# Two 256-column products in place of one 512-column product, per weight tile, in a float32 transformer trunk

## The chip, the cores and the metric

The kernel runs on one core of one Trainium2 chip. The metric is the device time of one execution in microseconds (us), lower is better. TensorE (PE) multiplies, and a matmul needs its stationary tile loaded first (the trace shows these loads as PEld). VectorE (DVE) and ScalarE (ACT) do the elementwise work, GpSimd (POOL) and SyncE (SP) issue the DMAs.

## The reference

Two decoder layers over 256 tokens of width 2048, all in float32. Layer 0 mixes tokens with attention with forget gates (16 heads of 128), layer 1 with a gated convolution of width 3. Each mixer is followed by a squared-ReLU MLP of width 8192, and each sub-layer has an RMSNorm, a shift and scale and a residual gate, which come from a conditioning vector `c`.

```python
for i in range(DEPTH):
    mod = c_act @ ada_w[i] + ada_b[i]
    sh_mix, sc_mix, g_mix, sh_mlp, sc_mlp, g_mlp = jnp.split(mod, N_MOD, axis=-1)
    h = modulate(rmsnorm(x, norm_mix[i]), sh_mix, sc_mix)
    mix = fox_mixer(...) if i % 2 == 0 else short_conv_mixer(...)
    x = x + g_mix[:, None, :] * mix
    h = modulate(rmsnorm(x, norm_mlp[i]), sh_mlp, sc_mlp)
    x = x + g_mlp[:, None, :] * sq_relu_mlp(h, mlp_w_up[i], mlp_w_down[i])
return rmsnorm(x, final_norm)
```

## The kernel before

All weights stream once from memory, so the matmuls are cut into 96 units. A unit is the product of 2048 input rows with 512 output columns of some weight matrix: 12 units for q, k and v, 4 for the attention output, 32 for the first MLP (4 slices of 4 up and 4 down units), 12 and 4 for the convolution mixer, 32 for the second MLP. Activations lie transposed, with features on the partitions and the 256 tokens in the columns.

To keep float32 accuracy with a faster number format (float32r), each number is split in a rounded high part and a low rest. For a weight chunk of 2 x 128 rows, ACT writes the high part (`w_hi`, line 598) and DVE the rest (`w_lo`, line 773). The ring of these chunks is four deep, and a unit has eight of them (`e` runs over them). The activations (`h`, `mid`) hold both parts side by side, 256 columns of the high part and then 256 of the low one. For each of the 16 k-steps of a unit and each of its 4 blocks of 128 output columns, `multiply` has two matmuls: `hi` times all 512 columns into a whole PSUM bank (line 370), and `lo` times the 256 high columns into the first half of this bank (line 372). That makes hi·hi + lo·hi in columns 0 to 255 and hi·lo in columns 256 to 511. These two are called the pair below. Four of the q, k, v units (v) are laid out the other way round, with `tokens_out`, and have three 512-column matmuls (lines 363 to 365).

The two halves of a bank are put together at the end of the unit. ACT copies the second half of its four banks to `tmp` (`half`, line 615, 1024 columns), and DVE adds it to the first half (`whole`, line 828 or 830). After this comes what the unit needs: the residual (ACT applies the gate, DVE adds to `xT`, ACT squares, DVE sums the squares), the squared ReLU, or the convolution. Two sets of four PSUM banks alternate, so that TensorE begins unit u when unit u-2 has been read (`evacuated`). ACT and DVE each have one order written out by hand, `body`: eight splits for the chunks ahead, between them pieces of the matrix-vector product with `ada_w` (DVE, line 785), then the evacuation. The first chunks of unit u+1 are split before unit u is evacuated.

The attention's own matmuls have up to 256 columns: `scores` (lines 486 to 490, ten matmuls for each head, of 256 and 128 columns) and `mix_values` (lines 509 to 511, six for each head). In both, one stationary tile is in part used by two matmuls in a row.

Of the kernel before, what the change touches and what calls it, by code (L numbers as in the profile page):

```python
# [1 line left out]

# [21 lines left out]
T = 256  # L24
# [42 lines left out]
def build(nc, x, c, ada_w, ada_b, norm_mix, norm_mlp, fox_w_in, fox_b_f, fox_w_out,  # L67
          conv_w_in, conv_w, conv_w_out, mlp_w_up, mlp_w_down, final_norm, out):
    ctx = ExitStack()
    with ctx:  # L70
# [103 lines left out]
        hi_ready = sem("hi_ready")  # L174
        split_ready = sem("split_ready")
        split_used = sem("split_used")
        half_ready = sem("half_ready")
        evacuated = sem("evacuated")
        ada_steps = sem("ada_steps")
        ada_summed = sem("ada_summed")  # L180
# [164 lines left out]
        def _(pe):  # L345
            mm = nc.tensor.matmul

            def multiply(u, par, rhs, ada=None, tokens_out=False, ready=None, after=None):


                pe.wait_ge(evacuated, u + 1)
                for e in range(NE):
                    pe.wait_ge(split_ready, NE * u + e + NE + 1)
                    if ready is not None:
                        ready(e)
                    for kk in range(EK):
                        k = EK * e + kk
                        hi, lo = w_hi[:, e % WR, kk, :], w_lo[:, e % WR, kk, :]
                        if tokens_out:
                            for a in range(TT):  # L360
                                o = ps[:, NB * par + a, :]
                                xh, xl = rhs[:, k, 0, P * a:P * (a + 1)], rhs[:, k, 1, P * a:P * (a + 1)]
                                mm(o, xh, hi, start=(k == 0), stop=False)  # L363
                                mm(o, xl, hi, start=False, stop=False)
                                last = mm(o, xh, lo, start=False, stop=(k == KC - 1))
                        else:
                            for j in range(NB):
                                cols = slice(P * j, P * (j + 1))

                                mm(ps[:, NB * par + j, :], hi[:, cols], rhs[:, k, :, :].rearrange("p s t -> p (s t)"),  # L370
                                   start=(k == 0), stop=False)
                                last = mm(ps[:, NB * par + j, 0:T], lo[:, cols], rhs[:, k, 0, :],  # L372
                                          start=False, stop=(k == KC - 1))
                    last.then_inc(split_used, 1)
                    if e == NE // 2 - 1 and ada is not None:
                        pe.wait_ge(evacuated, u + 2)

                        ada_sum(*ada, NB * par + NB - 1 if tokens_out else NB * (1 - par))
                    if after is not None and e in after:
                        after[e]()  # L380
# [209 lines left out]
        def _(act):  # L590
# [18 lines left out]
                act.wait_ge(split_used, NE * u + NE)  # L609
                evac()  # L610

            def half(u, par, scale=1.0, n_red=NQ):
                act.wait_ge(evacuated, u + 2)
                act.wait_ge(reduced, n_red)
                op(tmp, ps[:, NB * par:NB * (par + 1), T:2 * T], ACT.Copy, scale=scale).then_inc(half_ready, 1)  # L615

            def residual(u, par, gate0, k, n_res):
                half(u, par, n_red=NQ + n_res)
                act.wait_ge(evacuated, u + 3)
                for j in range(NB):  # L620
# [72 lines left out]
            for g in range(NG):  # L693
                for t in range(3):
                    u = 3 * g + t
                    par = u % 2

                    def evac():
                        if t == 2:
                            op(vs[:, :, 0, :], ps[:, NB * par:NB * par + TT, :], ACT.Copy).then_inc(qkv_hi, 1)  # L700
                        else:
                            half(u, par, SCALE if t == 0 else 1.0)
                            act.wait_ge(evacuated, u + 3)
                            op((qs, ks)[t][:, :, 0, :], fsum, ACT.Copy).then_inc(qkv_hi, 1)
                            if t == 1:
                                load_nf(g)
                    after = None
                    if t == 0 and g:
                        after = {1: lambda: round_attn(g - 1, NB * (1 - par) + 2)}
                    elif t == 1 and g == 0:  # L710
                        after = {1: forget_rows}
                    elif t == 2:
                        after = {0: lambda: exps(g, NB * (1 - par)), 2: lambda: round_probs(g, NB * (1 - par))}
                    body(u, evac, after=after)
# [4 lines left out]
            def mlp_slice(s, base, l, last=False):  # L719
                for n in range(NG):  # L720
                    u = base + 2 * NG * s + n

                    def evac():
                        half(u, n % 2, n_red=NQ + NG * (1 + l) + SLICES * NG * l + NG * s)
                        act.wait_ge(relu2, SLICES * NG * l + NG * s + n + 1)
                        op(mid[:, NB * n:NB * (n + 1), 0, :], fsum, ACT.Copy).then_inc(hid_hi, 1)  # L726
                    body(u, evac)
                for n in range(NG):
                    u = base + 2 * NG * s + NG + n
                    body(u, lambda: residual(u, n % 2, NROW * l + 5 * KC, NB * n,  # L730
                                             NG * (1 + l) + SLICES * NG * l + NG * s + n), more=not (last and n == NG - 1))
# [5 lines left out]
            with act.Fori(0, NG // 2) as r:  # L737
                for i in range(2):
                    g = 2 * r + i
                    for t in range(3):  # L740
# [1 line left out]
                        u = U_CONV + 6 * r + pos  # L742

                        def evac():
                            half(u, pos % 2, n_red=NQ + NG * (1 + SLICES))
                            if t == 2:
                                act.wait_ge(conv_in, g + 1)
                                act.wait_ge(conv_ready, g)
                                for j in range(NB):
                                    last = op(conv_y[:, j, :], conv_u[:, j, 0:T], ACT.Copy, scale=taps[:, ds(NB * g + j, 1)])  # L750
                                last.then_inc(conv_tap, 1)
                                act.wait_ge(conv_gated, g + 1)
                                op(mid[:, ds(NB * g, NB), 0, :], conv_y[:, :, :], ACT.Copy).then_inc(conv_hi, 1)
# [14 lines left out]
        def _(dve):  # L768
# [50 lines left out]
                for i in range(ada_late, NQ):  # L819
                    ada_quarter_of(i)  # L820

            def whole(u, par, dst, scale=1.0, n_half=None, used=()):

                for wait in used:
                    dve.wait_ge(*wait)
                dve.wait_ge(half_ready, n_half)
                if scale == 1.0:
                    v.tensor_tensor(dst, ps[:, NB * par:NB * (par + 1), 0:T], tmp, ALU.add).then_inc(evacuated, 1)  # L828
                else:
                    v.scalar_tensor_tensor(dst, ps[:, NB * par:NB * (par + 1), 0:T], scale, tmp,  # L830
                                           ALU.mult, ALU.add).then_inc(evacuated, 1)

            def residual(u, par, k, slot, n_half, n_res, used=()):
                whole(u, par, fsum, n_half=n_half, used=((added, n_res),) + used)
                dve.wait_ge(gated, n_res + 1)
                v.tensor_tensor(xT[:, ds(k, NB), :], xT[:, ds(k, NB), :], fsum, ALU.add).then_inc(added, 1)  # L836

# [171 lines left out]
            for g in range(NG):  # L1009
                for t in range(3):  # L1010
# [3 lines left out]
                    def evac():  # L1014
# [3 lines left out]
                                            vs[:, :, 0, :].bitcast(F32), ALU.subtract).then_inc(evacuated, 1)  # L1018
                        else:
                            dst = (qs, ks)[t]  # L1020
                            whole(u, par, fsum, SCALE if t == 0 else 1.0, n_half=2 * g + t + 1,
                                  used=((qkv_ready, 2 * g + t),))
                            dve.wait_ge(qkv_hi, 3 * g + t + 1)
                            v.tensor_tensor(dst[:, :, 1, :], fsum, dst[:, :, 0, :].bitcast(F32), ALU.subtract).then_inc(qkv_ready, 1)
# [10 lines left out]
                         ada_first=t == 2, ada_late=2 if t == 1 else NQ)  # L1035
            for n in range(NG):
                u = U_OUT0 + n
                body(u, lambda: residual(u, n % 2, NB * n, n, u - NG + 1, n),
                     (u + A_START, n % 2), (u + A_START - 1, NB * ((n + 1) % 2)),
                     after=None if n else {1: lambda: low_attn(NG - 1, NB + 2)})  # L1040

            def mlp_slice(s, base, l, adas, last=False):
                n_hid = SLICES * NG * l + NG * s
                n_add = NG * (1 + l) + n_hid
                for n in range(2 * NG):
# [2 lines left out]

                    def evac():
                        if n >= NG:  # L1050
                            residual(u, n % 2, NB * (n - NG), n - NG, u - NG + 1, n_add + n - NG, ((hid_ready, n_hid + NG),))
                            return
                        whole(u, n % 2, fsum, n_half=u - NG + 1, used=((hid_ready, n_hid + n), (added, n_add)))
                        dve.wait_ge(evacuated, u + 3)
                        v.scalar_tensor_tensor(fsum, fsum, 0.0, fsum, ALU.max, ALU.mult).then_inc(relu2, 1)  # L1055
                        dve.wait_ge(hid_hi, n_hid + n + 1)
# [14 lines left out]
            with dve.Fori(0, NG // 2) as r:  # L1071
                for i in range(2):
                    g = 2 * r + i
                    for t in range(3):
# [2 lines left out]
                        a = A_CONV + 4 * r + 2 * i + t  # L1077

                        def evac():
                            whole(u, pos % 2, (conv_b[:, :, :], conv_c[:, :, :], fsum)[t], n_half=u - NG + 1)  # L1080
                            if t == 2:
                                dve.wait_ge(evacuated, u + 3)
                                v.tensor_tensor(conv_u[:, :, 2:T + 2], conv_c[:, :, :], fsum, ALU.mult).then_inc(conv_in, 1)
# [12 lines left out]
                        body(u, evac, (a, t % 2) if t < 2 else None, (a - 1, NB * ((pos + 1) % 2)) if t else None)  # L1096
            for n in range(NG):
                u = U_OUT1 + n
                body(u, lambda: residual(u, n % 2, NB * n, n, u - NG + 1, NG * (1 + SLICES) + n))
            norm(3, MLP_GAIN[1], NROW + 3 * KC, A_END)  # L1100
            with dve.Fori(0, SLICES - 1) as s:
                mlp_slice(s, U_MLP1, 1, False)
# [28 lines left out]
```

## Time and profile before

| | |
|---|---|
| median of 3 runs | 2579.46 us (2575.14 to 2583.95) |
| span of the profiled execution | 2578.3 us, first to last instruction |
| PE busy | 2382.4 us, 92% |
| DVE busy | 1923.0 us, 75% |
| ACT busy | 1102.4 us, 43% |
| mean granted TensorE clock | 0.950 of full speed |
| read from memory | 606 MB, 236 GB/s over the span |

Durations of matmuls overlap in the trace: a matmul's record lasts until its results are written, and the next one has long begun. What a matmul costs in a stream is therefore the time from its start to the next one's start, which is called its step below. The profiled execution's own total time isn't given beside its span; its span lies 1.2 us under the median of the runs.

### The profile page before, as it was taken

What the parts mean: (1) busy time and instruction counts of PE and PEld (TensorE: products, weight loads), DVE (VectorE), ACT (ScalarE), POOL (GpSimd) and SP (SyncE); (2) the same over time, 40 slices, a digit from 0 to 9 for tenths busy, and PEclk for the clock granted to TensorE, in tenths of its full rate; (3) what the DMA queues carried; (4) which work ended last, traced back from release to release, by engine and by line L of the source; (5) the groups of instructions that cost most, each with busy time, mean ns of one, the idle gap of its engine ahead of it and who ended that gap; (6) DMA issues with size and microseconds to landing.
All of it is one profiled execution on the core that took longest, in us unless ns stands there. A gap on an engine that the chain in (4) does not pass through costs nothing.

```text
span 2578.3 us, 35741 instructions
## 1 busy us (share of the span) xinstructions
PE 2382.4 (92%) x13304; PEld 2075.5 (80%) x13304; DVE 1923.0 (75%) x2089; ACT 1102.4 (43%) x1252; POOL 148.3 (6%) x208
## 2 busy tenths in 40 slices
PE   4899998985999999999997999998899999999996
PEld 4887787774888888888886888887788888888885
DVE  6878889888877887887888888865756555565555
ACT  1044434434444454444444344344445445445452
POOL 2201011100000000000000000000000000000000
PEclk7589999997999999999998999999999999999998
DMA  8967798884887877878874887755455555655551
GB/s 306 340 240 271 273 323 297 279 292 165 287 282 253 271 271 265 277 262 271 271 270 162 315 298 271 265 177 194 130 181 188 179 173 196 187 189 180 185 175 66
DMA packets 259228, 610.80 MB, mean 237 GB/s; under 512 B 11656, under 2 KB 12024, under 8 KB 258816
## 3 DMA queue, kind: packets, MB, share of 16 engines
q1 hardware_dynamic: 206768, 407.18, 46.8%
q0 software_dynamic: 52224, 201.34, 22.5%
q8 instruction: 114, 1.87, 0.3%
q14 instruction: 42, 0.34, 0.0%
q10 hardware_dynamic: 80, 0.07, 0.0%
HBM read 606.42 MB, written 2.13 MB: 236 GB/s over the span
## 4 chain that ended last, share of the span: by engine, by line
PE 74%; DVE 14%; issue 4%; ACT 4%; DMA 3%; DVEq 0%; SPq 0%; ACTq 0%; POOLq 0%
PE ps L370 46%; PE ps L372 23%; DVE acc L785 5%; DMA ada_raw<-in_ada_w_dram 3%; DVE w_lo L773 3%; PE ps L438 1%; DVE scratch L828 1%; PE ps L386 1%; ACT w_hi L598 1%; DVE squares L843 1%; ACT scratch L621 1%; DVE scratch L948 1%; DVE h L956 1%; ACT h L649 1%; DMA xrow<-in_x_dram 1%
## 5 line engine op out<-in xcount | busy, mean ns | idle before, releaser
L370 PE MATMUL ps<-h,w_hi 128*128 128x512 f32 x3328 | 1189.7, 402 | 63.6 <-DVE h L956 22.5
L773 DVE TENSOR_TENSOR w_lo<-raw,w_hi 128x1024 fp32r<-128x1024 f32 x768 | 916.8, 1221 | 372.2 <-ACT w_hi L598 367.9
L598 ACT ACTIVATE w_hi<-raw 128x1024 fp32r<-128x1024 f32 x768 | 797.8, 1057 | 896.3 <-PE ps L372 894.9
L372 PE MATMUL ps<-h,w_lo 128*128 128x256 f32 x3328 | 939.2, 282 | 0.0
L370 PE MATMUL ps<-mid,w_hi 128*128 128x512 f32 x2560 | 908.9, 399 | 16.0 <-DVE w_lo L773 14.5
L370 PEld LDWEIGHTS ps<-h,w_hi 128*128 128x128 f32 x3328 | 633.5, 190 | 222.1 <-issue 46.7
L372 PE MATMUL ps<-mid,w_lo 128*128 128x256 f32 x2560 | 720.8, 282 | 0.0
L372 PEld LDWEIGHTS ps<-h,w_lo 128*128 128x128 f32 x3328 | 636.9, 191 | 0.0
L370 PEld LDWEIGHTS ps<-mid,w_hi 128*128 128x128 f32 x2560 | 484.1, 189 | 134.4 <-DVE w_lo L773 15.1
L372 PEld LDWEIGHTS ps<-mid,w_lo 128*128 128x128 f32 x2560 | 486.9, 190 | 0.0
L785 DVE SCALAR_TENSOR_TENSOR acc<-ada_raw,ca,acc 128x512 f32<-128x512 f32 x600 | 450.6, 751 | 34.6 <-DMA ada_raw<-in_ada_w_dram 17.0
L336 POOL DMA_DIRECT2D ada_raw<-in_ada_w_dram x160 | 120.4, 752 | 1450.6 <-DVE acc L785 1412.6
L843 DVE TENSOR_REDUCE squares<-scratch 128x256 f32<-128x1024 f32 x44 | 88.7, 2017 | 48.4 <-ACT scratch L624 45.1
L828 DVE TENSOR_TENSOR scratch<-ps,scratch 128x1024 f32<-128x1024 f32 x80 | 97.5, 1218 | 9.6 <-ACT scratch L615 9.6
L621 ACT ACTIVATE scratch<-scratch,mod 128x256 f32<-128x256 f32 x160 | 68.4, 498 | 81.7 <-DVE scratch L828 81.7
L836 DVE TENSOR_TENSOR xT<-xT,scratch 128x1024 f32<-128x1024 f32 x40 | 49.0, 1226 | 71.0 <-ACT scratch L621 71.0
L615 ACT ACTIVATE scratch<-ps 128x1024 f32<-128x1024 f32 x92 | 92.7, 1008 | 10.2 <-PE ps L372 10.2
L785 DVE SCALAR_TENSOR_TENSOR acc<-start_ring,ca,acc 128x512 f32<-128x512 f32 x90 | 67.6, 752 | 6.9 <-DMA start_ring<-in_ada_w_dram 2.8
L726 ACT ACTIVATE mid<-scratch 128x1024 fp32r<-128x1024 f32 x32 | 34.0, 1062 | 88.8 <-DVE scratch L1055 88.8
L649 ACT ACTIVATE h<-scratch 128x512 fp32r<-128x512 f32 x32 | 20.2, 632 | 110.9 <-DVE scratch L948 110.9
L363 PE MATMUL ps<-w_hi,h 128*128 128x512 f32 x128 | 53.7, 420 | 14.1 <-DVE w_lo L773 14.1
L395 PE MATMUL ps<-squares,ones 128*128 128x256 f32 x40 | 16.5, 546 | 54.2 <-DVE squares L843 45.8
(138 smaller groups left out, 1078.0 us busy)
## 6 DMA issues: line engine op xcount, KB each, us to landing
ada_raw<-in_ada_w_dram POOLq DMA_DIRECT2D x160, 1024.0 KB, 6.3
raw<-in_mlp_w_up_dram SPq DMA_DIRECT2D x128, 1024.0 KB, 5.6
raw<-in_mlp_w_down_dram SPq DMA_DIRECT2D x128, 1024.0 KB, 5.3
raw<-in_fox_w_in_dram SPq DMA_DIRECT2D x48, 1024.0 KB, 7.3
raw<-in_conv_w_in_dram SPq DMA_DIRECT2D x48, 1024.0 KB, 7.6
start_ring<-in_ada_w_dram POOLq DMA_DIRECT2D x32, 1024.0 KB, 9.1
raw<-in_fox_w_out_dram SPq DMA_DIRECT2D x16, 1024.0 KB, 7.5
raw<-in_conv_w_out_dram SPq DMA_DIRECT2D x16, 1024.0 KB, 5.2
```

Source lines behind the costliest of these rows:

```text
L336: pool.dma_start(ada_raw[:, q % 2], ada_quarter(layer, a - NMOD * NG * layer, q)).then_inc(ada_arrived[q % 2], 16)
L363: mm(o, xh, hi, start=(k == 0), stop=False)
L370: mm(ps[:, NB * par + j, :], hi[:, cols], rhs[:, k, :, :].rearrange("p s t -> p (s t)"), start=(k == 0), stop=False)
L372: last = mm(ps[:, NB * par + j, 0:T], lo[:, cols], rhs[:, k, 0, :], start=False, stop=(k == KC - 1))
L598: op(w_hi[:, e % WR], raw[:, e // 2, EK * (e % 2):EK * (e % 2 + 1)], ACT.Copy).then_inc(hi_ready, 1)
L615: op(tmp, ps[:, NB * par:NB * (par + 1), T:2 * T], ACT.Copy, scale=scale).then_inc(half_ready, 1)
L621: last = op(fsum[:, j, :], fsum[:, j, :], ACT.Copy, scale=mod[:, ds(gate0 + k + j, 1)])
L773: v.tensor_tensor(w_lo[:, e % WR], raw[:, e // 2, EK * (e % 2):EK * (e % 2 + 1)], w_hi[:, e % WR].bitcast(F32), ALU.subtract).then_inc(spl ...
L785: v.scalar_tensor_tensor(acc[:, slot, :], src[:, kk, :], ca[:, k:k + 1], acc[:, slot, :], ALU.mult, ALU.add).then_inc(ada_steps, 1)
L828: v.tensor_tensor(dst, ps[:, NB * par:NB * (par + 1), 0:T], tmp, ALU.add).then_inc(evacuated, 1)
L836: v.tensor_tensor(xT[:, ds(k, NB), :], xT[:, ds(k, NB), :], fsum, ALU.add).then_inc(added, 1)
L843: v.tensor_reduce(squares[:, m, :], tmp.rearrange("p k t -> p t k"), AX.X, ALU.add).then_inc(reduced, 1)
```

## The change

The 512-column matmul becomes two matmuls of 256 columns with the same stationary tile, both into columns 0 to 255. All three products are then summed in PSUM, in the same half of the bank; the other half is unused. `half` is gone with its semaphore, and `whole` reads the one half by itself and writes it out, times `scale`.

```diff
-  mm(ps[:, NB * par + j, :], hi[:, cols], rhs[:, k, :, :].rearrange("p s t -> p (s t)"),
-     start=(k == 0), stop=False)
+  mm(ps[:, NB * par + j, 0:T], hi[:, cols], rhs[:, k, 0, :], start=(k == 0), stop=False)
+  mm(ps[:, NB * par + j, 0:T], hi[:, cols], rhs[:, k, 1, :], start=False, stop=False)
   last = mm(ps[:, NB * par + j, 0:T], lo[:, cols], rhs[:, k, 0, :],
             start=False, stop=(k == KC - 1))
...
-  def half(u, par, scale=1.0, n_red=NQ):
-      act.wait_ge(evacuated, u + 2)
-      act.wait_ge(reduced, n_red)
-      op(tmp, ps[:, NB * par:NB * (par + 1), T:2 * T], ACT.Copy, scale=scale).then_inc(half_ready, 1)
...
   def residual(u, par, gate0, k, n_res):
-      half(u, par, n_red=NQ + n_res)
       act.wait_ge(evacuated, u + 3)
...
-  def whole(u, par, dst, scale=1.0, n_half=None, used=()):
+  def whole(u, par, dst, scale=1.0, used=()):
       for wait in used:
           dve.wait_ge(*wait)
-      dve.wait_ge(half_ready, n_half)
-      if scale == 1.0:
-          v.tensor_tensor(dst, ps[:, NB * par:NB * (par + 1), 0:T], tmp, ALU.add).then_inc(evacuated, 1)
-      else:
-          v.scalar_tensor_tensor(dst, ps[:, NB * par:NB * (par + 1), 0:T], scale, tmp,
-                                 ALU.mult, ALU.add).then_inc(evacuated, 1)
+      dve.wait_ge(split_used, NE * u + NE)
+      v.tensor_scalar(dst, ps[:, NB * par:NB * (par + 1), 0:T], scale, None, ALU.mult).then_inc(evacuated, 1)
```

The calls of `half` in the four evacuations of ACT and the argument `n_half` in those of DVE go with it. The four `tokens_out` units are unchanged.

## Rows read from the trace of the kernel before

**Rows 1.** Page, busy time: engine, us (share), instructions.

```profile
span 2578.3 us, 35741 instructions
...
PE 2382.4 (92%) x13304; PEld 2075.5 (80%) x13304; DVE 1923.0 (75%) x2089; ACT 1102.4 (43%) x1252; POOL 148.3 (6%) x208
```

**Rows 2.** Page, the chain that ended last, by line.

```profile
PE ps L370 46%; PE ps L372 23%; DVE acc L785 5%; DMA ada_raw<-in_ada_w_dram 3%; DVE w_lo L773 3%; PE ps L438 1%; DVE scratch L828 1%; PE ps L386 1%; ACT w_hi L598 1%; DVE squares L843 1%; ACT scratch L621 1%; DVE scratch L948 1%; DVE h L956 1%; ACT h L649 1%; DMA xrow<-in_x_dram 1%
```

**Rows 3.** Groups by line and shape: xcount, busy us, mean ns, idle before.

```profile
L370 PE MATMUL ps<-h,w_hi 128*128 128x512 f32 x3328 | 1189.7, 402 | 63.6 <-DVE h L956 22.5 <-DVE w_lo L773 22.3 <-issue 8.3
L370 PE MATMUL ps<-mid,w_hi 128*128 128x512 f32 x2560 | 908.9, 399 | 16.0 <-DVE w_lo L773 14.5 <-issue 1.5
...
L828 DVE TENSOR_TENSOR scratch<-ps,scratch 128x1024 f32<-128x1024 f32 x80 | 97.5, 1218 | 9.6 <-ACT scratch L615 9.6
...
L848 DVE TENSOR_SCALAR var<-ps 128x256 f32<-128x256 f32 x5 | 2.1, 423 | 7.5 <-PE ps L395 7.5
...
L853 DVE TENSOR_TENSOR newton<-inv 128x256 f32<-128x256 f32 x5 | 2.1, 426 | 2.4 <-ACT inv L640 1.9 <-ACT inv L634 0.5
...
L615 ACT ACTIVATE scratch<-ps 128x1024 f32<-128x1024 f32 x92 | 92.7, 1008 | 10.2 <-PE ps L372 10.2
```

**Rows 4.** Line 370 alone in four stretches: A:B, us, PE busy (count), PEld busy (count), clock, DMA.

```profile
650.00:800.00 150.00, 147.70 (x421) 78.77 (x421) 1.00 0.82 280
1220.00:1370.00 150.00, 147.71 (x422) 78.90 (x421) 1.00 0.80 270
1850.00:1990.00 140.00, 140.00 (x397) 74.46 (x397) 1.00 0.56 183
2210.00:2310.00 100.00, 100.00 (x289) 54.03 (x289) 1.00 0.57 184
```

**Rows 5.** PE's timeline, the pair in the stream: start us, duration us.

```profile
1200.24 0.40 PE L370 MATMUL ps<-h,w_hi 128*128 128x512 f32 x1
...
1200.48 0.28 PE L372 MATMUL ps<-h,w_lo 128*128 128x256 f32 x1
...
1200.59 0.40 PE L370 MATMUL ps<-h,w_hi 128*128 128x512 f32 x1
```

**Rows 6.** PE's timeline, attention scores of head group 3.

```profile
461.71 0.33 PE L486 MATMUL ps<-ks,qs 128*128 128x256 f32 x1
...
462.40 0.27 PE L487 MATMUL ps<-ks,qs 128*128 128x128 f32 x1
...
462.73 0.28 PE L490 MATMUL ps<-causal,ident_r 128*128 128x128 f32 x1
...
463.99 0.33 PE L486 MATMUL ps<-ks,qs 128*128 128x256 f32 x1
```

**Rows 7.** PE's timeline, attention values of head group 3.

```profile
500.77 0.34 PE L509 MATMUL ps<-qs,vs 128*128 128x256 f32 x1
...
502.14 0.45 PE L370 MATMUL ps<-mid,w_hi 128*128 128x512 f32 x1
```

**Rows 8.** PE's timeline in a v unit, only 512-column matmuls, ten steps apart.

```profile
470.36 0.39 PE L363 MATMUL ps<-w_hi,h 128*128 128x512 f32 x1
...
472.63 0.39 PE L364 MATMUL ps<-w_hi,h 128*128 128x512 f32 x1
```

**Rows 9.** ACT's and DVE's timeline around the end of one unit.

```profile
789.17 1.06 ACT L598 ACTIVATE w_hi<-raw 128x1024 fp32r<-128x1024 f32 x1 [1.71 <-PE ps L372]
790.14 1.01 ACT L615 ACTIVATE scratch<-ps 128x1024 f32<-128x1024 f32 x1
...
790.27 1.23 DVE L773 TENSOR_TENSOR w_lo<-raw,w_hi 128x1024 fp32r<-128x1024 f32 x1 [0.16 <-ACT w_hi L598]
791.41 1.22 DVE L828 TENSOR_TENSOR scratch<-ps,scratch 128x1024 f32<-128x1024 f32 x1
```

**Rows 10.** Timeline after the last unit.

```profile
2545.96 1.02 ACT L615 ACTIVATE scratch<-ps 128x1024 f32<-128x1024 f32 x1 [10.25 <-PE ps L372]
```

**Rows 11.** Waits: who waited for whom, us in total, times, longest.

```profile
PE ps L370 <- DVE w_lo L773: 36.9, 11, 4.3
...
PE ps L370 <- DVE scratch L828: 7.6, 2, 3.9
```

More of the change, by code:

```diff
@@ L176, in build @@
         split_used = sem("split_used")
-        half_ready = sem("half_ready")
         evacuated = sem("evacuated")
@@ L701, in evac @@
                         else:
-                            half(u, par, SCALE if t == 0 else 1.0)
                             act.wait_ge(evacuated, u + 3)
@@ L723, in evac @@
                     def evac():
-                        half(u, n % 2, n_red=NQ + NG * (1 + l) + SLICES * NG * l + NG * s)
                         act.wait_ge(relu2, SLICES * NG * l + NG * s + n + 1)
@@ L744, in evac @@
                         def evac():
-                            half(u, pos % 2, n_red=NQ + NG * (1 + SLICES))
                             if t == 2:
@@ L820, in body, with residual @@
                     ada_quarter_of(i)
-            def whole(u, par, dst, scale=1.0, n_half=None, used=()):
+            def whole(u, par, dst, scale=1.0, used=()):
                 for wait in used:
                     dve.wait_ge(*wait)
-                dve.wait_ge(half_ready, n_half)
-                if scale == 1.0:
-                    v.tensor_tensor(dst, ps[:, NB * par:NB * (par + 1), 0:T], tmp, ALU.add).then_inc(evacuated, 1)
-                else:
-                    v.scalar_tensor_tensor(dst, ps[:, NB * par:NB * (par + 1), 0:T], scale, tmp,
-                                           ALU.mult, ALU.add).then_inc(evacuated, 1)
-            def residual(u, par, k, slot, n_half, n_res, used=()):
-                whole(u, par, fsum, n_half=n_half, used=((added, n_res),) + used)
+                dve.wait_ge(split_used, NE * u + NE)
+                v.tensor_scalar(dst, ps[:, NB * par:NB * (par + 1), 0:T], scale, None, ALU.mult).then_inc(evacuated, 1)
+            def residual(u, par, k, slot, n_res, used=()):
+                whole(u, par, fsum, used=((added, n_res),) + used)
                 dve.wait_ge(gated, n_res + 1)
@@ L1020, in evac @@
                             dst = (qs, ks)[t]
-                            whole(u, par, fsum, SCALE if t == 0 else 1.0, n_half=2 * g + t + 1,
+                            whole(u, par, fsum, SCALE if t == 0 else 1.0,
                                   used=((qkv_ready, 2 * g + t),))
@@ L1037, in _ @@
                 u = U_OUT0 + n
-                body(u, lambda: residual(u, n % 2, NB * n, n, u - NG + 1, n),
+                body(u, lambda: residual(u, n % 2, NB * n, n, n),
                      (u + A_START, n % 2), (u + A_START - 1, NB * ((n + 1) % 2)),
@@ L1050, in evac @@
                         if n >= NG:
-                            residual(u, n % 2, NB * (n - NG), n - NG, u - NG + 1, n_add + n - NG, ((hid_ready, n_hid + NG),))
+                            residual(u, n % 2, NB * (n - NG), n - NG, n_add + n - NG, ((hid_ready, n_hid + NG),))
                             return
-                        whole(u, n % 2, fsum, n_half=u - NG + 1, used=((hid_ready, n_hid + n), (added, n_add)))
+                        whole(u, n % 2, fsum, used=((hid_ready, n_hid + n), (added, n_add)))
                         dve.wait_ge(evacuated, u + 3)
@@ L1079, in evac @@
                         def evac():
-                            whole(u, pos % 2, (conv_b[:, :, :], conv_c[:, :, :], fsum)[t], n_half=u - NG + 1)
+                            whole(u, pos % 2, (conv_b[:, :, :], conv_c[:, :, :], fsum)[t])
                             if t == 2:
@@ L1098, in _ @@
                 u = U_OUT1 + n
-                body(u, lambda: residual(u, n % 2, NB * n, n, u - NG + 1, NG * (1 + SLICES) + n))
+                body(u, lambda: residual(u, n % 2, NB * n, n, NG * (1 + SLICES) + n))
             norm(3, MLP_GAIN[1], NROW + 3 * KC, A_END)
```

## The prediction

> **What bounds the kernel.** I read the busy shares first, then the chain that ended last, then the groups by line, and last the timelines, because the records of matmuls overlap and their durations say little. PE is busy for 92% of the span and no other engine for more than 80% [rows 1]; the chain lies on the pair of lines 370 and 372 for 69% of the span [rows 2]. There are 3328 + 2560 = 5888 pairs [rows 3]. So the question is what one pair costs in the stream, and what three shorter matmuls cost in its place. All else is small against 5888 times a few nanoseconds: 1 ns per pair is 5.9 us, and a difference of 0.3%, about what a measurement of this kernel can tell from none, is 7.7 us or 1.3 ns per pair.
>
> **What a pair costs.** In four stretches at full granted clock line 370 began 421, 422, 397 and 289 times in 147.7, 147.7, 140.0 and 100.0 us of its own busy time, which for an overlapping stream is the time it fills [rows 4]. That is 0.351, 0.350, 0.353 and 0.346 us per pair. All four together: 535.4 / 1529 = 0.350 us. There are two paces, 0.353 (third stretch) and 0.346 (fourth), and nothing in their DMA share (0.56 and 0.57) tells them apart. 768 columns at one column per cycle of 2.4 GHz are 0.320 us, so 26 to 33 ns of a pair aren't columns. In the timeline the 512-column matmul takes a step of 0.24 and the 256-column one of 0.11 [rows 5].
>
> **What the change adds on PE.** Per pair, one matmul and one weight load more, with the same 768 columns: 5888 matmuls and 5888 loads more. Loads stand one to one beside matmuls before (13304 of each, rows 1), also where two in a row have the same tile, so the second half's load isn't saved. The third matmul is free only if all that lies between two matmuls is hidden behind columns. The cost is that of three steps of 256 columns. I take it from the places where 256-column matmuls follow each other:
>
> - Scores: two heads' worth, from 461.71 to 463.99, hold 2 x 10 matmuls, 2 x 4 of 256 columns and 2 x 6 of 128; per head 1.140 us. Three steps between 128-column matmuls take 462.73 - 462.40 = 0.33, so 0.110 each, or 0.112 with the rounding of the rows [rows 6]. (1.140 - 6 x 0.112) / 4 = 0.117, and with 0.110 it is 0.120.
> - Values: from 500.77 to 502.14 there are two heads of 3 + 3 matmuls, 0.685 per head [rows 7]. (0.685 - 3 x 0.112) / 3 = 0.116; with 0.110 it is 0.118. Here the order is the changed one: high tile, high tile again, low tile.
>
> I take 0.118, in the middle of 0.116 to 0.120, because these are the same operation with the same tile sizes. Three of them are 0.354 us, against 0.350: +4 ns per pair.
>
> Both bounds are far. Below: a 128-column matmul with its load takes 0.110 [rows 6], more than twice its columns' 0.053, so it is the load or the issue that sets it, and nothing goes below this; three are 0.330, -20 ns per pair or -118 us. Above: ten 512-column steps take 2.27 us, 0.227 each [rows 8], 13.7 ns over their columns. If each matmul had this whatever its size, three would cost 0.320 + 0.041 = 0.361, +11 ns; with the pair's own excess at its slower pace, 33 ns / 2 = 16.7 per matmul, it would be 0.370, +20 ns or +118 us. The short step of line 372 in the pair, 0.11 to 0.12 [rows 5], would make 0.345, -5 ns, but part of that step may be booked to its neighbour of 0.24.
>
> Here a rule can be laid beside the row. The row says that a 512-column matmul takes 0.227 us in a stream [rows 8]. The Trainium skill, page "TensorE: Matmul & The Clock Gate", section "Back-to-back issue gap", gives columns / 2.4 plus 2.5 ns, so 0.216, which the row exceeds by 11 ns. By the page one more matmul per pair would cost 2.5 ns or +15 us, as an estimate; its section on loading the stationary operand gives 107 ns for 128 columns, as long as a 256-column matmul's columns, which speaks against this change, since such a load has no spare cover. The trace agrees with the load's figure: 0.110 a step at 128 columns.
>
> **How many pairs pay.** Where PE waits for DVE's `w_lo` in any case, slower matmuls eat into the wait. There are 11 such waits of 36.9 us together [rows 11], one for one unit each; I take half of the 64 pairs of each as covered, 350. 5888 - 350 = 5540 pairs x 4 ns = +22 us.
>
> **What it removes.** 92 copies on ACT of 1.008 us [rows 3], 92.7 us of work, but beside the path. At the end of a unit ACT first does the last split (to 790.23), then the copy (790.14 to 791.15), while DVE splits the same chunk (790.27 to 791.50) and only then adds (791.41) [rows 9]. The copy is done before DVE could use it. All adds together have waited 9.6 us for the copy, once [rows 3]: after the last unit, where there are no further splits. There the copy of 1.02 us is on the path [rows 10] and goes away: -1 us. At nothing I cost the other 91, hidden by DVE's own split; without this cover they would cost 1 us each on the residual chain. ACT has 57% idle time, so its freed time isn't needed.
>
> The add becomes a scaling of 1024 columns out of PSUM on DVE. At 256 columns a `TENSOR_SCALAR` from PSUM takes 423 ns and a `TENSOR_TENSOR` 426 [rows 3], so I take the same 1.22 us and 0 for the difference; should it run shorter, it would be 92 times some tenths, off the path in the MLP units. Its wait moves from the copy to the last matmul of the unit, which is earlier. Behind it on DVE are the splits of the next unit, and they gain nothing since DVE comes to it late.
>
> `evacuated` comes no later, so PE's wait for a free bank (7.6 us in two waits, rows 11) stays. More instructions on PE must be fetched after each loop's jump; I put that at +0 to +3 us and leave it out of the sum.
>
> **Sum.** +22 - 1 = +21 us. The span would go from 2578.3 to 2599; the median of the runs is 1.2 us above the span, so 2600 us.
>
> **The rivals.**
>
> 1. *A fixed price per matmul.* If handing over from one stationary tile to the next costs as much at 256 columns as at 512, a triple is 0.360 to 0.370 and the time 2579 + (10 to 17 ns x 5888 = 59 to 100) = 2640 to 2680. For it speaks that 512-column steps (13.7 ns over) and the pair (26 to 33 over for two matmuls) fit the same price; against it that 256-column steps in attention are only 10 to 13 over. Also in this class: the attention's runs are 40 matmuls long, and a sustained stream of 17 loads and matmuls per us, where the pair has 11, is shown nowhere; if PE can't be fed at this rate for long, it costs here.
> 2. *Short steps (faster).* In the pair the 256-column matmul's step is 0.11 to 0.12, and what hangs over may belong to the 512-column one. If all three take 0.115, a triple is 0.345, and the time 2579 - 5 x 5888 = 2550. It decides below 0.1167 (0.350 / 3). For it speaks row group 5; against it that in attention, where sums over whole heads leave nothing to be booked to a neighbour, I find 0.116 to 0.120.
> 3. *Columns alone count.* The excess is in proportion to the columns: 0.350 / 768 per column, the triple costs what the pair costs, and only the copy at the end is left: 2575 to 2586. Rows 8 speak against it: 0.227 for 512 columns is less per column than the pair.
>
> **How the numbers follow.** Forecast (triple 0.352 to 0.357, +10 to +40 us) 0.42; rival 1 0.20; rival 2 0.21; rival 3 0.17. Slower is 0.42 + 0.20 = 0.62, faster 0.21, the same 0.17. The predicted time is 2600, its own range 2589 to 2619. The range for 8 in 10 takes in rival 3, rival 2 down to 2552 and the lower part of rival 1, to 2655; outside are 0.08 of rival 2 and 0.10 of rival 1.
>
> **What the profile after would show.** PE with 13304 + 5888 = 19192 matmuls and as many loads. In the stream, one step of about 0.118 after the other and 0.354 per block of three; 0.345 shows rival 2, 0.360 and more rival 1. ACT's busy time down by 93 us, DVE's unchanged within 5 us with the new group at 1.2 us. The evacuation begins at the same distance from the unit's last matmul as before, except after the last unit, where it comes 1 us sooner. I would be wrong in kind if the stalls between units changed by more than some us in sum.

## The result, and the profile after

The changed kernel takes 2656.8 us (2654.4 to 2658.7, 4 runs) against 2581.1 (2575.1 to 2584.0) of the kernel before: slower by 3.1%, ratio 1.0308, 95% interval 1.0285 to 1.033. The way was forecast; the size, +21 us, was less than a third of the 76 us measured, and 2656.8 lies just over the range of 2552 to 2655. The span went from 2578.3 to 2654.9 us, +76.6.

The page of the changed kernel: busy time, then the chain that ended last by line, then groups by line (what each writes and reads, count, busy us, mean ns, idle time before).

```profile
span 2654.9 us, 47284 instructions
...
PE 2444.0 (92%) x19192; PEld 2410.0 (91%) x19192; DVE 1924.6 (72%) x2089; ACT 1017.4 (38%) x1160; POOL 147.8 (6%) x208
...
PE ps L359 25%; PE ps L360 25%; PE ps L361 25%; DVE acc L765 3%; DMA ada_raw<-in_ada_w_dram 2%; PE ps L427 1%; DVE scratch L807 1%; PE ps L375 1%; ACT w_hi L587 1%; DVE w_lo L753 1%; DVE squares L819 1%; DVE scratch L924 1%; DVE h L932 1%; ACT h L632 1%; DMA xrow<-in_x_dram 1%
...
L359 PE MATMUL ps<-h,w_hi 128*128 128x256 f32 x3328 | 959.5, 288 | 72.7 <-issue 29.5
L360 PE MATMUL ps<-h,w_hi 128*128 128x256 f32 x3328 | 955.4, 287 | 9.0 <-issue 9.0
...
L807 DVE TENSOR_SCALAR scratch<-ps 128x1024 f32<-128x1024 f32 x84 | 102.3, 1218 | 8.9 <-PE ps L361 8.9
```

The three matmuls are now lines 359 to 361, `whole` is line 807. PE has the 19192 matmuls and as many loads. VectorE is unchanged in sum, and its new evacuation takes 1.218 us like the add that it replaces [rows 3]; ACT has lost the 92 copies. The chain lies on the three matmuls for 75% of a longer span. Two things have grown against [rows 1, 3]: the weight loads are busy for 91% of the span, nearly as long as the matmuls, where it was 80%, and idle time named "issue" before the matmuls is 29.5 + 9.0 us, where it was 8.3 + 1.5.

The stream itself, PE's timeline:

```profile
2622.75 0.28 PE L359 MATMUL ps<-mid,w_hi 128*128 128x256 f32 x1
2622.87 0.28 PE L360 MATMUL ps<-mid,w_hi 128*128 128x256 f32 x1
...
2622.99 0.28 PE L361 MATMUL ps<-mid,w_lo 128*128 128x256 f32 x1
...
2623.11 0.28 PE L359 MATMUL ps<-mid,w_hi 128*128 128x256 f32 x1
...
2623.23 0.28 PE L360 MATMUL ps<-mid,w_hi 128*128 128x256 f32 x1
```

Every step is 0.120, and three are 0.360 us. The two paces of the pair [rows 4] are gone.

And one jump back of TensorE's loop over the slices, in the second MLP. First the kernel before, then the changed one (timeline of PE; the square bracket is the idle time before):

```profile
1997.71 0.28 PE L372 MATMUL ps<-mid,w_lo 128*128 128x256 f32 x1
1998.97 0.47 PE L370 MATMUL ps<-h,w_hi 128*128 128x512 f32 x1 [0.98 <-issue]
...
2001.97 0.50 PE L370 MATMUL ps<-h,w_hi 128*128 128x512 f32 x1 [1.03 <-issue]
```

```profile
2043.43 0.55 PE L359 MATMUL ps<-h,w_hi 128*128 128x256 f32 x1 [4.67 <-issue]
...
2045.07 0.41 PE L360 MATMUL ps<-h,w_hi 128*128 128x256 f32 x1
2045.28 0.41 PE L361 MATMUL ps<-h,w_lo 128*128 128x256 f32 x1
2045.49 0.41 PE L359 MATMUL ps<-h,w_hi 128*128 128x256 f32 x1
2049.19 0.58 PE L360 MATMUL ps<-h,w_hi 128*128 128x256 f32 x1 [3.28 <-issue]
```

2.0 us of idle time at this jump have become 8.0, in two parts, and the steps between are 0.21: TensorE is at the lower of its two clocks, 1.2 GHz. Four stretches of 23 us of the changed kernel show what that makes (A:B, us, busy and count of PE, PEld, DVE, ACT, POOL, granted clock, DMA): one without a jump, and the three that hold a jump of the second MLP.

```profile
1998.00:2021.00 23.00, 23.00 (x194) 23.00 (x193) 13.81 (x12) 10.91 (x13) 0.00 (x0) 1.00 0.55 180
2038.00:2061.00 23.00, 15.04 (x101) 14.57 (x100) 9.38 (x8) 6.99 (x9) 0.00 (x0) 0.78 0.32 97
2233.00:2256.00 23.00, 15.66 (x108) 15.19 (x107) 9.84 (x8) 6.99 (x9) 0.00 (x0) 0.78 0.35 108
2428.00:2451.00 23.00, 15.56 (x107) 15.09 (x107) 9.55 (x8) 7.12 (x10) 0.00 (x0) 0.78 0.34 110
```

Against 194 matmuls there are 93, 86 and 87 too few, 266 x 0.120 = 32 us in three jumps. The idle time in them is 23 us (8.0, 7.3 and 7.5); the other 9 are matmuls at the lower clock. Before, the stretch at such a jump had full clock, and about 13 of 131 matmuls too few, 2 us:

```profile
1997.00:2020.00 23.00, 20.99 (x118) 17.75 (x117) 13.34 (x11) 10.88 (x13) 0.00 (x0) 1.00 0.56 177
```

The jumps of the first MLP look otherwise. There the kernel before idles for 3.9, 3.4 and 3.7 us too, and the changed one for 5.5, 5.8 and 4.9. In the kernel before these stalls don't stand under "issue" but under the name of a wait for VectorE:

```profile
815.24 0.47 PE L370 MATMUL ps<-h,w_hi 128*128 128x512 f32 x1 [3.88 <-DVE scratch L828]
```

### The profile page after: what moved, and what is told of

Same layout as the page of the kernel before. It is cut to its first block, busy times and chain, and to the rows that moved or that the text cites. A ratio compares the mean times of both kernels' runs of the same rounds, so it can differ in the third digit from the quotient of the medians.

```text
span 2654.9 us, 47284 instructions
## 1 busy us (share of the span) xinstructions
PE 2444.0 (92%) x19192; PEld 2410.0 (91%) x19192; DVE 1924.6 (72%) x2089; ACT 1017.4 (38%) x1160; POOL 147.8 (6%) x208
## 4 chain that ended last, share of the span: by engine, by line
PE 81%; DVE 10%; ACT 3%; issue 3%; DMA 2%; SPq 0%; DVEq 0%; ACTq 0%; POOLq 0%
PE ps L359 25%; PE ps L360 25%; PE ps L361 25%; DVE acc L765 3%; DMA ada_raw<-in_ada_w_dram 2%; PE ps L427 1%; DVE scratch L807 1%; PE ps L375 1%; ACT w_hi L587 1%; DVE w_lo L753 1%; DVE squares L819 1%; DVE scratch L924 1%; DVE h L932 1%; ACT h L632 1%; DMA xrow<-in_x_dram 1%
## 5 line engine op out<-in xcount | busy, mean ns | idle before, releaser
L359 PE MATMUL ps<-h,w_hi 128*128 128x256 f32 x3328 | 959.5, 288 | 72.7 <-issue 29.5
L360 PE MATMUL ps<-h,w_hi 128*128 128x256 f32 x3328 | 955.4, 287 | 9.0 <-issue 9.0
L361 PE MATMUL ps<-h,w_lo 128*128 128x256 f32 x3328 | 954.4, 287 | 0.0
L359 PE MATMUL ps<-mid,w_hi 128*128 128x256 f32 x2560 | 728.3, 284 | 15.1 <-DVE w_lo L753 14.4
L360 PE MATMUL ps<-mid,w_hi 128*128 128x256 f32 x2560 | 726.7, 284 | 0.0
L359 PEld LDWEIGHTS ps<-h,w_hi 128*128 128x128 f32 x3328 | 653.2, 196 | 78.1 <-issue 64.9
L360 PEld LDWEIGHTS ps<-h,w_hi 128*128 128x128 f32 x3328 | 653.1, 196 | 9.8 <-issue 9.8
L361 PEld LDWEIGHTS ps<-h,w_lo 128*128 128x128 f32 x3328 | 652.5, 196 | 0.0
L359 PEld LDWEIGHTS ps<-mid,w_hi 128*128 128x128 f32 x2560 | 493.9, 193 | 15.9 <-DVE w_lo L753 14.9
L360 PEld LDWEIGHTS ps<-mid,w_hi 128*128 128x128 f32 x2560 | 494.0, 193 | 0.0
L361 PEld LDWEIGHTS ps<-mid,w_lo 128*128 128x128 f32 x2560 | 493.8, 193 | 0.0
L807 DVE TENSOR_SCALAR scratch<-ps 128x1024 f32<-128x1024 f32 x84 | 102.3, 1218 | 8.9 <-PE ps L361 8.9
```

Of the source, the lines that this page charges most:

```text
L359: mm(ps[:, NB * par + j, 0:T], hi[:, cols], rhs[:, k, 0, :], start=(k == 0), stop=False)
L360: mm(ps[:, NB * par + j, 0:T], hi[:, cols], rhs[:, k, 1, :], start=False, stop=False)
L807: v.tensor_scalar(dst, ps[:, NB * par:NB * (par + 1), 0:T], scale, None, ALU.mult).then_inc(evacuated, 1)
```

## The experiments

The questions: is 0.120 the price of every matmul, and of what is it made; has the evacuation a part in the time; and how much of the 77 us lies at the jumps. "Theory A" and "B" have their own meaning in each expectation. Ratios are against the kernel before in the same series; its median was 2581.1, 2576.7 and 2577.2 us in the three series, and 2574.4 in a single run beside runs 7 to 9. The changed kernel itself ran only in the first.

**1. The step by itself.** A kernel that only runs streams of matmuls (shortened here; `s(n)` picks one of eight stationary tiles of 128 columns), for each stream:

```diff
+  for n in range(96):
+      mm(ps[:, n % 4, 0:N], w[:, s(n)], m[:, 0:N], start=True, stop=True)   # N = 512 ... 64
...
+  for n in range(64):
+      mm(ps[:, n % 4, 0:256], w[:, s(n)], m[:, 0:256], start=True, stop=False)
+      mm(ps[:, n % 4, 0:256], w[:, s(n)], m[:, 256:512], start=False, stop=False)
+      mm(ps[:, n % 4, 0:256], w[:, s(n + 4)], m[:, 0:256], start=False, stop=True)
```

> This kernel leaves the whole model out: it copies x to the output and runs streams of about 100 matmuls with nothing beside them, each stream with one number of moving columns (512, 448, 384, 320, 288, 256, 240, 224, 192, 128, 64), every matmul with its own weight load, all at float32r; then the pair of 512 and 256, the triple of 256, bfloat16 streams of 512, 256 and 128, and a triple cut as 384, 128 and 256. It measures the step alone. Theory A, a fixed price per matmul beside its columns: step = columns / 2.4 + 13.3 ns, so 0.227, 0.200, 0.173, 0.147, 0.133, 0.120 down to 256, and still falling below it (0.113 at 240, 0.107 at 224), until the load's own length stops it at 0.110; bfloat16 at 256 columns stays near 0.120. Theory B, at 256 columns the weight load and not the columns sets the step: the steps are flat at 0.120 from 256 (or even 288) columns downwards, and bfloat16, whose load is shorter, falls to about 0.109 at 256. The cut 384 + 128 + 256 would cost 0.360 by A with a load that can run ahead, and 0.40 or more by B.

Streams of it by line: count, shortest, median and longest duration in ns, first and last start in us, form. The step is (last start - first start) / (count - 1).

```profile
L61 PE MATMUL ps<-m,w x96: 389/389/389, 29.6 to 51.1; 128*128 128x512 f32 x96
```

```profile
L69 PE MATMUL ps<-m,w x96: 333/334/346, 76.2 to 92.7; 128*128 128x384 f32 x96
```

```profile
L81 PE MATMUL ps<-m,w x160: 277/283/283, 127.9 to 147.0; 128*128 128x256 f32 x160
```

```profile
L85 PE MATMUL ps<-m,w x96: 270/274/278, 149.8 to 160.4; 128*128 128x240 f32 x96
```

```profile
L97 PE MATMUL ps<-m,w x96: 220/275/280, 190.2 to 200.8; 128*128 128x128 f32 x96
```

```profile
L114 PE MATMUL ps<-mb,wb x96: 272/273/273, 290.0 to 300.4; 128*128 128x256 bf16 x96
```

```profile
L116 PE MATMUL ps<-mb,wb x96: 219/219/219, 300.5 to 305.8; 128*128 128x128 bf16 x96
```

```profile
L118 PE MATMUL ps<-m,w x64: 336/338/418, 305.8 to 331.5; 128*128 128x384 f32 x64
```

21.5 / 95 = 0.226 at 512 columns, 16.5 / 95 = 0.174 at 384, 19.1 / 159 = 0.120 at 256, 10.6 / 95 = 0.112 at 240 and the same at 128. With full float32r tiles the step is columns / 2.4 plus about 13 ns at 512, 384 and 256 columns, and 0.112 from 240 columns down to 128. So at 256 the step is still above the load's floor, and theory A holds for the sizes that the kernel uses. It fails in two places. In bfloat16 a 256-column matmul takes 10.4 / 95 = 0.109, 2 to 3 ns over its columns, and a 128-column one with a full load 5.3 / 95 = 0.056: both the 13 ns and the floor of 0.112 belong to float32r and not to any matmul. And the triple cut in 384 + 128 + 256 took 0.408 (25.7 us for 63 of them), as B said. That is the sum of the three single steps, 0.174 + 0.112 + 0.120 = 0.406: the long matmul doesn't make up for the short one.

The pair isn't such a sum. Alone, it took 22.2 / 63 = 0.352 (223.7 to 245.9 us), while 0.226 + 0.120 is 0.346. So a third matmul costs 7 or 8 ns beside the pair, and not the 13 of a single matmul. Why the pair costs 6 or 7 ns more than its parts isn't shown.

One stream shows the clock. With 64 columns the steps were 0.112, and in the middle of the stream, without any idle time of TensorE, they became 0.213, as the granted clock in the last but two columns of these stretches fell from 1.00 to 0.50 (the counts take in matmuls cut by a stretch's ends):

```profile
204.00:209.00 5.00, 5.00 (x47) 5.00 (x47) 0.00 (x0) 0.00 (x0) 1.00 0.02 3
209.50:218.50 9.00, 9.00 (x44) 9.00 (x44) 0.00 (x0) 0.00 (x0) 0.50 0.00 0
```

**2. The same, finer.** More column counts, smaller stationary tiles, long runs.

```diff
+  for n in range(96):
+      mm(ps[0:64, n % 4, 0:256], w[:, P * (n % 8):P * (n % 8) + 64], m[:, 0:256], start=True, stop=True)
...
+  for n in range(480):
+      ...   # the triple of run 1
```

> Again the whole model is left out: x is copied to the output beside streams of matmuls at float32r. Streams of 272 to 232 moving columns find where the load's floor begins: by columns / 2.4 + 13.3, 0.127, 0.123, 0.120, 0.117, 0.113, then 0.111 flat. With stationary tiles of 64 and 32 columns: if the 13.3 ns belongs to the load's length it shrinks (256 columns: 0.113 and 0.110; 512: 0.220 and 0.217); if it belongs to the change of tile as such, 0.120 and 0.227 stay, and only the floor falls (128 columns: from 0.111 to about 0.067). The same stationary tile every time: 0.120 if a reload of the same tile costs like any other, 0.109 if not. One bank instead of four: 0.120. Then 480 triples and 480 pairs in straight-line code: 0.360 and 0.347 to 0.353 throughout, without stalls, if TensorE can be fed with 17 instructions per us where nothing jumps.

```profile
L85 PE MATMUL ps<-m,w x96: 387/392/398, 113.7 to 135.6; 128*64 128x512 f32 x96
```

```profile
L89 PE MATMUL ps<-m,w x96: 275/276/282, 138.5 to 149.3; 128*64 128x256 f32 x96
```

```profile
L93 PE MATMUL ps<-m,w x96: 220/222/225, 152.2 to 157.9; 128*64 128x128 f32 x96
```

```profile
L101 PE MATMUL ps<-m,w x96: 279/281/282, 185.7 to 196.9; 128*32 128x256 f32 x96
```

```profile
L109 PE MATMUL ps<-m,w x96: 278/283/284, 208.4 to 219.8; 128*128 128x256 f32 x96
```

```profile
L117 PE MATMUL ps<-m,w x480: 278/283/284, 236.9 to 409.3; 128*128 128x256 f32 x160
```

```profile
L121 PE MATMUL ps<-m,w x480: 394/398/404, 409.7 to 578.9; 128*128 128x512 f32 x160
```

With a tile of 64 columns the step at 256 columns is 10.8 / 95 = 0.114, with 32 columns 11.2 / 95 = 0.118. At 512 columns shorter loads made it longer, 21.9 / 95 = 0.231 with 64 and 0.232 with 32, against 0.226. So neither alternative of the expectation came out: the excess doesn't follow the load's length, and it isn't one fixed price either. At 128 columns the step falls from 0.112 to 5.7 / 95 = 0.060 with the half tile and stays at 0.060 with the quarter: the floor of 0.112 is the load. The steps between the sizes of run 1 are not on one line: 248 columns took 0.115, but 264 took 0.120 like 256, only 10 ns over its columns. One bank in place of four changed nothing, 0.120. Loading the same tile each time (line 109) costs 0.120 like any other, so the second load of the same tile isn't cheaper. 480 triples in straight-line code take 172.4 / 479 = 0.360 without a gap: TensorE can be fed with 17 loads and matmuls per us. 480 pairs took 169.2 / 479 = 0.353.

**3. The matmuls alone.** The kernel before, its matmul cut in two halves, each into its own half of the bank, with copy and add kept.

```diff
-  mm(ps[:, NB * par + j, :], hi[:, cols], rhs[:, k, :, :].rearrange("p s t -> p (s t)"),
-     start=(k == 0), stop=False)
+  mm(ps[:, NB * par + j, 0:T], hi[:, cols], rhs[:, k, 0, :], start=(k == 0), stop=False)
+  mm(ps[:, NB * par + j, T:2 * T], hi[:, cols], rhs[:, k, 1, :], start=False, stop=False)
```

> The kernel before with the 512-column matmul cut in two of 256 columns, each into its own half of the bank; ACT's copy and DVE's add stay. Theory A, the time went to the extra matmul and load alone: steps of 0.120, the same longer stalls after loop jumps, 2657 to 2660 us, which is the changed kernel plus 1 us for the copy after the last unit. Theory B, something in the new evacuation or in three sums into the same columns costs a part: this kernel lies clearly between the two, 2600 to 2640.

2657.1 us, ratio 1.0312 (1.0279 to 1.0345): all of the loss, and theory A. The long stalls at the jumps are there too: 5.3, 4.2 and 5.3 us in the first MLP, 7.5, 7.2 and 7.7 in the second.

**4. The evacuation alone.** The changed kernel with the 512-column matmul of before; the second half of the banks isn't read, so the sums lack one of the three products.

> The kernel before with its 512-column matmul, but with the changed evacuation: no copy by ACT, and DVE scales the first half of the banks alone. This leaves the product of the weights' high part with the activations' low part out of the sums. Theory A, the copy was hidden: 2576 to 2581 us, 1 us less than before and not more. Theory B, freeing 93 us of ACT and one hand-over per unit shortens the stalls: 5 us or more faster, 2575 or less.

2577.0 us against 2576.7, ratio 1.0005 (0.9987 to 1.0022). The copy on ACT was free, as the prediction said; the 1 us at the very end is less than this can tell. Theory A.

**5 and 6. No jumps on TensorE.** In the kernel before and in the changed one, the three loops of TensorE's program are written out; those of the other engines stay.

```diff
-  with pe.Fori(0, SLICES) as s:
+  for s in range(0, SLICES):
...
-  with pe.Fori(0, NG // 2) as r:
+  for r in range(0, NG // 2):
```

> The kernel before with TensorE's three kinds of loop (MLP slices, two in the convolution mixer) written out, so that TensorE's program has no jump; the loops of the other engines stay. Theory A, the stalls of PE at the slice boundaries are the jump and the fetch behind it: the 17 us of gaps at six boundaries and the half clock behind them go away, 2555 to 2571 us against 2577. Theory B, these stalls are DVE's or ACT's own loop jumps: nothing changes, within 4 us of before.

> The changed kernel with the same loops written out. Theory A, its longer stalls after jumps (39 us in six places against 17 before) are instruction fetch, which runs dry sooner at 17 instead of 11 instructions per us: they go away, 2610 to 2632 us; over the unrolled kernel before only the steps are left, 5500 pairs x 9 ns = 50 us. Rival: at this rate the fetch runs dry without jumps too, new stalls named issue stand within the units, and the time is 2640 or more.

Before, written out: 2563.1 us, ratio 0.9946 (0.9927 to 0.9965), 14 us faster, with an interval of 9 to 19. Changed, written out: 2604.8, ratio 1.0105 (1.0081 to 1.013), 52 us faster than the changed kernel in its own series. For both, theory A; the changed one comes out below the 2610 to 2632 that I expected, and 42 us above the other in place of 50. In the stretch that held three jumps there is now not one gap:

```profile
1900.00:2500.00 600.00, 600.00 (x5002) 600.00 (x5001) 351.15 (x287) 261.59 (x283) 0.00 (x0) 1.00 0.54 183
```

600 us and 5002 matmuls are 0.120 each, at full clock, while the weights stream. So the rival, a fetch that runs dry without jumps, is out.

The waits named VectorE at the jumps of the first MLP change as well. With the loops written out, the kernel before waits there for 1.9, 1.2 and 2.0 us, in place of 3.9, 3.4 and 3.7, and no longer for `scratch` of line 828.

In the second MLP neither of the two waits for anything, so here pair and triple can be laid side by side, by the count of their first matmuls (lines 370 and 359) in 650 us:

```profile
1850.00:2500.00 650.00, 650.00 (x1841) 345.75 (x1840) 1.00 0.57 186
```

```profile
1850.00:2500.00 650.00, 511.02 (x1806) 346.61 (x1806) 1.00 0.54 184
```

That is 0.353 for the pair and 0.360 for the triple, 7 ns. Over the whole kernel before without jumps, the steps from pair to pair that hold no wait are 0.3516 on average, and the triple costs 8.3 ns more.

**7. Where the loop's code lies.** 128 idle waits before each MLP's loop in the changed kernel.

```diff
+  for _ in range(128):
+      pe.wait_ge(const_ready, 12)
   norm_sum(i)
   with pe.Fori(0, SLICES) as s:
```

> The changed kernel with 128 idle wait instructions put before each MLP's loop on TensorE, where it waits for VectorE anyway. They move the loop's code by 8 KB, half of one 16 KB block of instructions as the instruction queue's transfers show them. Theory P, where the loop's ends lie in such blocks sets the stall after a jump: the stalls of the second MLP (8.0, 7.3, 7.4 us in two parts) change by 2 us or more each. Theory R, the shorter matmuls leave less time ahead in which the next block can come: the stalls stay within 1 us.

2649.2 us in one run, 5 us below the lowest of the changed kernel's four. In the second MLP the second part of each stall (3.3, 2.7 and 3.0 us) is gone; the first part stays, here 4.64 us:

```profile
2044.65 0.55 PE L359 MATMUL ps<-h,w_hi 128*128 128x256 f32 x1 [4.64 <-issue]
```

So theory P for the second part: it hangs on where the code lies. It doesn't explain the first part, and the stalls of the first MLP stayed within 0.9 us.

**8 and 9. Two slices per iteration**, in the changed kernel and in the one before: one jump per MLP instead of three, a body twice as long.

```diff
-  with pe.Fori(0, SLICES) as s:
-      for n in range(2 * NG):
+  with pe.Fori(0, SLICES // 2) as s2:
+      for half_s in range(2):
+          s = 2 * s2 + half_s
+          for n in range(2 * NG):
```

> The changed kernel with two slices of the MLP in each iteration of TensorE's loop: one jump back per MLP instead of three, the body twice as long. If the cost is per jump, 4 of 6 jumps and two thirds of the 39 us of stalls go away, and with the 52 us that writing everything out gave, 2615 to 2628 us. If a longer body makes the stall longer (the changed body is 1.5 times the one before), the two jumps left cost 10 us or more each.

> The same for the kernel before: a body longer than the changed kernel's. If a body's length sets the stall, the one jump of the second MLP costs 6 us or more where it cost 2 to 2.5; if not, about 2.5, and the whole is 2562 to 2572.

2618.3 and 2570.1 us, one run each, both as expected if the cost is per jump. The first is 38 us below the changed kernel and clear of noise. The second is only 4 us below the kernel before, whose single executions lie between 2566.5 and 2584.5, so its time alone decides nothing; its trace does. The jump left in the second MLP, first of the changed kernel's variant, then of the other:

```profile
2214.81 0.55 PE L359 MATMUL ps<-h,w_hi 128*128 128x256 f32 x1 [4.30 <-DVE scratch L809]
```

```profile
2173.92 0.47 PE L370 MATMUL ps<-h,w_hi 128*128 128x512 f32 x1 [1.05 <-issue]
```

The body of the second is longer than the changed kernel's own, and its stall is still 1.05: the body's length doesn't set it. The first stands under another name, since a wait for VectorE lies at the same place; with all loops written out it is gone, so I count it as the same stall.

## Why the prediction was wrong

Taken apart by the runs, in spans: the two kernels without jumps are 2603.2 - 2559.8 = 43.4 us apart. That is what the matmuls cost. The jumps cost 2654.9 - 2603.2 = 51.7 us in the changed kernel and 2578.3 - 2559.8 = 18.5 in the one before: 33.2 more. Together they are the 76.6. These are single executions; by the medians of their series the three numbers are 42, 52 and 14, so the split is good to about 5 us.

- **The price of a triple, the first term that was mis-sized.** I took 0.354, from short runs in attention where 256- and 128-column matmuls alternate, against 0.350 for the pair: 4 ns. Measured: 0.360 in the stream and 0.360 alone, against 0.352 for the pair on average, so 8 ns. The pair was right, the triple wasn't. My way of splitting a head in 128-column steps of 0.110 to 0.112 and a rest gave 0.116 to 0.120 for the 256-column step; the truth is at its upper end, and 2 ns per step are 35 us. The timeline of the same head had it. Inside the head the starts of 256-column matmuls follow each other at 0.12:

```profile
461.87 0.28 PE L487 MATMUL ps<-ks,qs 128*128 128x256 f32 x1
461.99 0.28 PE L488 MATMUL ps<-ks,qs 128*128 128x256 f32 x1
462.11 0.28 PE L489 MATMUL ps<-nf_row,ones_r 128*128 128x256 f32 x1
462.23 0.22 PE L490 MATMUL ps<-causal,ident_r 128*128 128x128 f32 x1
462.29 0.28 PE L486 MATMUL ps<-ks,qs 128*128 128x128 f32 x1
```

  Where the sizes change, the starts are 0.16 (461.71 to 461.87, rows 6) and 0.06 (462.23 to 462.29) apart. These two steps together are less than 0.112 + 0.120, and my division put what they save on all 256-column steps. Rows 8 also had the figure: 13.7 ns over the columns, whatever the size, gave 0.361, and I put it down as a bound. Rival 1 in its lower half has the triple and the total of 2657 right, but the total by luck: it has 10 ns on every pair and no jumps, where the runs show 8 ns and the jumps. What I put beside it, that TensorE can't be fed 17 loads and matmuls per us for long, is refuted by runs 2 and 6.
- **Fetch after a jump, the second.** "I put that at +0 to +3 us and leave it out of the sum" failed: +33 us. The idle time at the six jumps of the MLPs went from 17.0 to 39.0 us, 22 of the 33. In the second MLP it went from 2 to 8 us per jump, and behind the longer stalls TensorE's granted clock fell to 1.2 GHz, which the idle time of 1 us before had not caused: the windows show 0.78 of the clock against 1.00. Part of what jumps cost before was in my rows under another name. The 7.6 us that I took for a wait for a free bank [rows 11] are the stalls at the first and the third jump of the first MLP; with the loops written out, only 1.9 and 2.0 us remain there, for `w_lo`. "I would be wrong in kind if the stalls between units changed by more than some us in sum" was the right test.
- **Pairs that don't pay.** 8.3 ns x 5888 is 49 us, and 43 were measured. Of the difference, 4.7 us are shown: PE's waits for `w_lo` are 52.7 us in the kernel before without jumps and 48.0 in the changed one. I had 350 pairs as covered; 4.7 us at 8.3 ns are some 570.
- **Right.** The copy hidden by VectorE's own split (run 4), the same 1.218 us for the scaling, 19192 matmuls and loads, the reload of the same tile at full price (run 2), and that the three products can be summed in one place at no cost or gain (run 3). The -1 us for the last copy is less than run 4 can tell.
- **The rule.** The Trainium skill's columns / 2.4 + 2.5 ns ("TensorE: Matmul & The Clock Gate", "Back-to-back issue gap"; it gives this for a matmul by itself) holds here for bfloat16, 0.109 at 256 columns and 0.216 at 512, and not for float32r, 0.120 and 0.226. The 107 ns that the Trainium skill gives there under "LDWEIGHTS (loading the stationary operand)" for 128 columns fits the floor of 0.112 in float32r; in bfloat16 a matmul of 128 columns with such a load took 0.056, so there it doesn't fit.

**What stays open.** Why a block of instructions comes late at some jumps and not at others. The trace shows transfers of an instruction queue in blocks of 16 KB; it doesn't say which engine they serve. The first of these two answers is the kernel before, the 8 us up to a jump of the second MLP, the second the changed kernel, the 4.5 us after the last matmul:

```profile
q8 instruction: 2, 0.03, 1.5%
```

```profile
q8 instruction: 1, 0.02, 1.3%
```

In the kernel before, the second of these blocks begins 1.5 us before the last matmul of the body; in the changed kernel none comes between 3.0 us before it and 2.2 us after it. What ties the stalls to the blocks is when they end. In the traces of the seven kernels with loops, the first matmul after each jump of the MLPs that idled starts 1.7 to 2.0 us after the end of such a block, under whatever name the stall stands, and the second part of a stall ends 1.2 to 1.6 us after one. In the changed kernel the block runs from 2040.72 to 2041.69 and the matmul starts at 2043.43; at the jump of the kernel before in the first MLP it runs from 812.01 to 813.47 and the matmul starts at 815.24. So in these traces the length of a first stall is how late its block is. Shorter matmuls alone don't explain the lateness: the first jump of run 4, with the matmuls of the kernel before, idled 4.6 us. A body of longer matmuls at the same instruction count wasn't tried.

## What to carry to other kernels

The price of a matmul in a stream is that of its columns plus a part that hangs on the number format, about 13 ns here in float32r. Take it from a long stream of the very sequence that you mean to run, not from a short mixed run and not as a sum of single prices: the sum was right for 384 + 128 + 256 and 7 ns too low for 512 + 256. Here the fewer and wider matmuls won although they need an extra copy of their result, since another engine had the time and the copy was hidden: 92 us of copies cost nothing and 5888 matmuls more cost 43. And count jumps, also those whose idle time stands under the name of a wait: in this kernel the loops of TensorE cost 14 to 18 us, and 52 with three matmuls in place of two. Writing the loops out made the kernel before faster by 14 us, to 2563.1, the lowest median of the versions run.

## What the runs showed of the hardware that I had not expected

- Full float32r tiles take about 13 ns per matmul over their columns (0.226 at 512, 0.120 at 256); bfloat16 takes 2 to 3. The excess isn't the load's length: at 256 columns 0.114 with a tile of 64 columns and 0.118 with 32, at 512 columns 0.231 and 0.232. At the lower clock there is none: the steps of 0.213 after the jump are 256 columns at 1.2 GHz.
- A float32r load of 128 columns is a floor of 0.112 for the step at full clock and of 0.213 at half clock (64 moving columns, run 1); with a tile of 64 columns the step goes down to 0.060.
- An idle time of 4.7 us at a jump was followed by a fall of TensorE's clock to 1.2 GHz, two of 1.0 us with 2 us between them were not. The clock also fell in the stream of 64-column matmuls, where TensorE had no idle time.
- A jump in the second MLP's loop costs TensorE 2 us or 8 us of idle time, by the matmuls in it and by the place of its code. The stall ends 1.7 to 2.0 us after an instruction block has come.
